# Forming the S5 way-in matrix in its final layout from turned B and repeated powers, in a one-layer hybrid encoder kernel

## Chip, cores and metric

One core of one Trainium2 chip runs the whole kernel. The metric is the device time of one execution in microseconds (us). Each kernel is run several times, and the median of the runs is its time.

## The reference

One encoder layer and a final RMS norm over 256 tokens of width 1024, all in f32. Cut to what matters here:

```python
q, k, v, u, g_a, g_s = split(rms_norm(h) @ w_in)          # 512 columns each for q, k, v, u; 1024 for g_a, g_s
o_a = diff_attention(rope(q), rope(k), v)                  # 4 heads, two softmaxes per head
o_s = s5_mixer(u)                                          # below
h = h + (sigmoid(g_a) * (o_a @ w_ba) + sigmoid(g_s) * (o_s @ w_bs)) @ w_mix_out
h = h + cross_attention(rms_norm(h), rms_norm(mem))        # 256 memory tokens
h = h + moe(rms_norm(h))                                   # top 4 of 32 experts, weights of 12.6 MB an expert

# s5_mixer, for each of 32 groups of 16 channels, 64 complex states, two directions:
ab = exp(a * dt); bb = ((ab - 1) / a) * b                  # bb: states x 16 channels
x[l] = ab * x[l-1] + bb @ u[l];  y[l] = real(c @ x[l])     # forward, and the same backward
```

## The kernel before

The kernel is written engine by engine: a block for SP (`block.sync`), for POOL (`block.gpsimd`), for PE, ACT and DVE, each a list of instructions in a fixed order. Semaphores tie them together, and nothing reorders an engine's list. So an instruction that waits holds up all that stands behind it on its engine.

Dense layers: a weight matrix comes in slabs of 512 columns. SP loads each in pieces of 512 rows (1 MB) into four slots of the tile `stage` (L307), and starts piece i when PE has used piece i-4 (`s_used`). The order is u, q, k, v, ga0, ga1, gs0, gs1 (the gates), mk0, mk1, mv0, mv1 (keys and values of the memory), and on to xo1. `natural` (L471) and `flipped` (L484) multiply a slab, in two layouts of the result. The results stand in four PSUM units PA to PD; `take` waits until the unit's last readers are done.

S5 works on chunks of 8 time steps: inside a chunk by a Toeplitz matrix (`toep`), between the 32 chunks by a scan on DVE. What a chunk adds to the state is `u` times the **way-in matrix** `lin`: for each group g a matrix of 128 rows (8 steps by 16 channels) and 256 columns (real and imaginary part of 128 states). Its entry is a power of `ab` for the step times `bb` for the channel. Before the change it is formed in five pieces of work:

1. `bbar` (states on partitions) from b and c by six DVE operations (L1366 to L1371), after rope of q and k.
2. For each of the 8 steps, six elementwise operations of 128x512 (`way_in_step`, L214) multiply `bbar` by one power into `s5b`, with the states on the partitions: 5 steps on DVE (`way_in`, L1405), 3 on POOL behind its own 48 operations for `s5w` (L399 to L404).
3. 64 transposes on PE (L460) turn `s5b`, 8 a PSUM unit. The units are PB and PD in turn.
4. ACT and DVE copy each turned unit back into the same place of `ring`, where it is now `lin`.
5. PE multiplies by it (L678).

In the same stretch PE runs the attention heads between the gate slabs: `scores(h)` (L596), then a gate slab during which DVE takes the row maxima (`row_max`, L1389), ACT the exponentials (`exps`, L1064) and DVE weighs the two softmaxes (`weigh`, L1394); then `turn_probs(h)` waits for `weigh(h)` (semaphore `pwv`), and `values(h)` for ACT's copy (`copy_probs`). The heads' order on PE is: scores 0, ga1, turn 0, scores 1, gs0, values 0, turn 1, scores 2, gs1, values 1, turn 2, scores 3, the matmuls of the taps (L654), values 2, the 64 transposes with turn 3 among them, values 3. `mem` is loaded by POOL after gs1 and normed into the tile of the first norm (`mn`).

On the DVE's list the way-in steps stand between the heads:

```python
            way_in(range(0, 1))
            for h, times in enumerate((range(1, 2), range(2, 3), range(3, WAY_IN_SPLIT), ())):
                row_max(h)
                weigh(h)
                if h == 0:
                    lag0()
                way_in(times)
```

`lag0` (L1414) forms the taps of lag 0 from a product of PE (L629). Behind the way-in matrix come the products (L678), their transposes, and the scan on DVE, which has to be done before PE's L719. From mk0 on the order of the program isn't touched by the change. The second half of the time is the mixture of experts: SP loads 192 chunks of 2 MB into a ring of 10 places, each when PE has used the chunk that was in its place.

## Time and profile before

| | us |
|---|---|
| median of 3 runs | 1316.97 |
| lowest and highest run | 1314.39, 1320.17 |
| the profiled execution, its own time | 1319.71 |
| its span, first to last instruction | 1317.9 |
| PE busy | 1262.1 (96%) |
| DVE, ACT, POOL busy | 348.2, 168.5, 109.6 |

The profile is of one execution. An engine's busy time says how long it worked, not whether it was waited for; the chain of waits says what released each piece of work up to the last. Times of day in the text are us from the span's start.

### The profile page before, as it was taken

The page shows a single profiled execution, that of the slowest core. Times are in us where ns is not written, and L with a number is a line of the kernel's source. Part 1 is how long each engine was busy: PE and PEld are TensorE (multiplying, and loading weights), DVE is VectorE, ACT ScalarE, POOL GpSimd, SP SyncE. Part 2 cuts the span into 40 slices and gives each one's busy share as a digit, 9 for nine tenths or more (in the row PEclk, how much of TensorE's full clock was granted, in tenths as well). Part 3 has the DMA queues.
Part 4 walks back from the last instruction along what each step waited for, and adds up shares of the span by engine and source line. Part 5 has one row for each costly group of instructions (what it writes and reads, how often), then busy time and mean ns, then how long its engine had stood idle before and what let it go on. Part 6 is the DMA issues. An engine that isn't in the chain of part 4 may idle for free.

```text
span 1317.9 us, 15237 instructions
## 1 busy us (share of the span) xinstructions
PE 1262.1 (96%) x6175; PEld 571.9 (43%) x6175; DVE 348.2 (26%) x754; ACT 168.5 (13%) x296; POOL 109.6 (8%) x108
## 2 busy tenths in 40 slices
PE   8999899999899999999999999999999999999996
PEld 3488785868653333333333333333333233333332
DVE  6578681121122111211122111211111112111112
ACT  2032422100311000000000000000000000000001
POOL 4699200010000000000000000000000000000000
PEclk9999999999989999999999999999999999999999
DMA  9633653549848999999999999999999999999994
GB/s 250 166 129 128 146 96 130 170 134 382 328 150 346 429 415 428 428 428 428 426 427 428 429 429 429 427 427 429 429 430 429 428 427 428 429 429 429 429 426 176
DMA packets 54984, 456.31 MB, mean 346 GB/s; under 512 B 4744, under 2 KB 6864, under 8 KB 30368
## 3 DMA queue, kind: packets, MB, share of 16 engines
q1 hardware_dynamic: 51744, 449.75, 82.9%
q0 software_dynamic: 2048, 5.47, 2.6%
q10 hardware_dynamic: 1152, 0.52, 0.3%
q8 instruction: 30, 0.49, 0.2%
q14 instruction: 10, 0.08, 0.0%
HBM read 453.59 MB, written 1.61 MB: 345 GB/s over the span
## 4 chain that ended last, share of the span: by engine, by line
PE 68%; DMA 23%; DVE 4%; ACT 3%; issue 1%; SPq 0%; ACTq 0%; DVEq 0%
PE pt L929 21%; PE pt L970 13%; DMA ring<-in_w_e 10%; DMA stage<-in_w_e 7%; DMA low<-in_w_e 6%; PE pt L493 6%; PE pt L480 6%; PE pt L528 4%; PE pt L866 4%; PE pt L460 3%; PE pt L851 3%; PE pt L541 2%; PE pt L923 1%; ACT wi_ L1008 1%; DMA stage<-in_w_in 1%; ACT low L1071 1%
## 5 line engine op out<-in xcount | busy, mean ns | idle before, releaser
L929 PE MATMUL pt<-ring,a 128*64 128x512 f32 x1216 | 273.0, 595 | 11.8 <-DMA ring<-in_w_e 11.7
L929 PEld LDWEIGHTS pt<-ring,a 128*64 128x64 f32 x1216 | 84.3, 137 | 193.4 <-issue 166.8
L970 PE MATMUL pt<-ring,wi_ 128*64 128x512 f32 x640 | 141.7, 595 | 4.6 <-ACT wi_ L1008 4.6
L1567 DVE COPY ct_<-ct_ 128x2 f32 x32 | 5.4, 170 | 468.7 <-PE pt L929 467.4
L929 PE MATMUL pt<-stage,a 128*64 128x512 f32 x416 | 95.3, 604 | 5.3 <-DMA stage<-in_w_e 5.3
L929 PE MATMUL pt<-low,a 128*64 128x512 f32 x416 | 93.8, 595 | 4.4 <-DMA low<-in_w_e 4.4
L970 PEld LDWEIGHTS pt<-ring,wi_ 128*64 128x64 f32 x640 | 44.6, 137 | 88.0 <-issue 82.0
L1184 ACT ACTIVATE hnt<-pt 128x512 f32<-128x512 f32 x32 | 19.1, 597 | 479.2 <-PE pt L929 479.2
L1644 DVE TENSOR_SCALAR hnt<-pt 128x512 f32<-128x512 f32 x32 | 22.1, 692 | 188.9 <-PE pt L929 188.9
L866 PE MATMUL pt<-hnt,lamb 64*128 64x512 f32 x256 | 65.3, 629 | 0.7 <-ACT hnt L1008 0.7
L851 PE MATMUL pt<-hres,ct_ 128*64 128x512 f32 x256 | 60.4, 592 | 0.0
L929 PEld LDWEIGHTS pt<-stage,a 128*64 128x64 f32 x416 | 29.1, 138 | 69.0 <-issue 58.4
L929 PEld LDWEIGHTS pt<-low,a 128*64 128x64 f32 x416 | 28.7, 137 | 67.3 <-issue 57.6
L480 PE MATMUL pt<-stage,hnt 128*128 128x512 f32 x128 | 55.3, 593 | 2.0 <-DMA stage<-in_w_in 2.0
L493 PE MATMUL pt<-hnt,stage 128*128 128x256 f32 x256 | 55.9, 379 | 0.0
L493 PEld LDWEIGHTS pt<-hnt,stage 128*128 128x128 f32 x256 | 48.6, 190 | 6.5
L1008 ACT ACTIVATE hnt<-pt 128x512 f32<-128x512 f32 (+1 forms) x34 | 21.1, 622 | 235.4 <-PE pt L970 230.3
L970 PE MATMUL pt<-low,wi_ 128*64 128x512 f32 x192 | 42.5, 595 | 1.3 <-ACT wi_ L1008 1.3
L970 PE MATMUL pt<-stage,wi_ 128*64 128x512 f32 x192 | 42.5, 595 | 1.3 <-ACT wi_ L1008 1.3
L1594 DVE TENSOR_TENSOR a<-pt,gains 128x512 f32<-128x512 f32 (+1 forms) x34 | 23.0, 676 | 70.2 <-PE pt L460 70.2
L480 PEld LDWEIGHTS pt<-stage,hnt 128*128 128x128 f32 x128 | 24.2, 190 | 31.8 <-issue 29.4
L923 PE MATMUL pt<-uT_,ct_ 32*64 32x512 f32 x256 | 34.8, 613 | 2.2 <-DMA low<-in_w_e 0.8
(325 smaller groups left out, 1215.4 us busy)
## 6 DMA issues: line engine op xcount, KB each, us to landing
ring<-in_w_e SPq DMA_DIRECT2D x116, 2048.0 KB, 35.9
low<-in_w_e SPq DMA_DIRECT2D x38, 2048.0 KB, 38.2
stage<-in_w_e SPq DMA_DIRECT2D x38, 2048.0 KB, 35.7
stage<-in_w_in SPq DMA_DIRECT2D x16, 1024.0 KB, 7.0
stage<-in_w_xkv SPq DMA_DIRECT2D x8, 1024.0 KB, 5.7
stage<-in_w_mix_out SPq DMA_DIRECT2D x4, 1024.0 KB, 5.1
stage<-in_w_xq SPq DMA_DIRECT2D x4, 1024.0 KB, 5.3
stage<-in_w_xo SPq DMA_DIRECT2D x4, 1024.0 KB, 16.5
```

The costliest lines, as they stand in the source:

```text
L460: return pe.transpose(dst, src, ident[0:n, 0:n])
L480: last = pe.matmul(pt[u][:, 512 * t:512 * t + 512], xT[:, k, t * P:(t + 1) * P], w[:, k % 4, :], start=(k == 0), stop=(k == 4 * len(ws) - 1))
L493: last = pe.matmul(pt[u][:, L * m:L * m + L], w[:, k % 4, m * P:(m + 1) * P], xT[:, k, :], start=(k == 0), stop=(k == 4 * len(ws) - 1))
L528: last = pe.matmul(pt[u][:, 512 * n:512 * (n + 1)], xT[:, k, P * t:P * (t + 1)], w[:, k % 4, :], start=(k == 0), stop=(k == KD - 1))
L541: last = pe.matmul(pt[u][:, L * m + P * t:L * m + P * (t + 1)], w[:, k % 4, m * P:(m + 1) * P], xT[:, k, P * t:P * (t + 1)], start=(k == 0 ...
L851: last = pe.matmul(pt[PD][SLOTS * n:SLOTS * (n + 1), 0:512], sel[:, t, :], h3[:, t, 512 * n:512 * (n + 1)], start=(t == 0), stop=(t == NT ...
L866: last = pe.matmul(pt[(PA, PB)[t]][:, 512 * n:512 * (n + 1)], gsc[SLOTS * n:SLOTS * (n + 1), t], ysb[SLOTS * n:SLOTS * (n + 1), :], start= ...
L923: pe.matmul(pt[PC][SLOTS * g:SLOTS * (g + 1), 512 * b:512 * (b + 1)], ecol[i:i + NE, :], be1[i:i + NE, :], start=False, stop=False)
L929: last = pe.matmul(pt[PC][SLOTS * g:SLOTS * (g + 1), 512 * b:512 * (b + 1)], xT[:, k % 4, k // 4], ring_slot[n][:, c:c + 512], start=(k == ...
L970: last = pe.matmul(pt[PD][SLOTS * h:SLOTS * (h + 1), 512:1024], hT[:, c, g], ring_slot[n][:, D * c + 512 * h:D * c + 512 * (h + 1)], start ...
L1008: return act.activation(dst, src, ACT.Copy)
L1594: return dve.tensor_tensor(xT[:, lo:hi], src, g3[:, lo:hi].to_broadcast([P, hi - lo, 2, SLOTS]), ALU.mult)
```

## The change

The way-in matrix is formed where PE wants it, with steps and channels on the partitions:

- **B turned once.** PE turns `bbar` (8 transposes, `turn_b`, into PD) in the middle of slab v, ACT copies it out (`b_turned`), and SP writes it to DRAM (`b_dram`, 0.5 MB).
- **Powers in row form.** The powers already stand on 32 partitions (one for each group). DVE copies them into order (`way_in_powers`, 4 copies and 4 memsets, behind rope of q), and SP writes them to DRAM in four transfers (`lam_dram`, 64 KB each), waits, and loads them back with **one DMA of 4 MB onto all 128 partitions**, straight into `lin`: each row of 32 KB is repeated on 16 partitions. That DMA stands ahead of ga0's pieces.
- **B repeated by DMAs.** Four loads of 1 MB (`load_b`) bring a quarter of turned B each, the same 16 rows repeated for the 8 steps, into two places of `ring`. The first two stand ahead of ga1's pieces, behind the write of `b_dram`; the third and fourth wait for quarters 1 and 2 of the matrix.
- **24 DVE operations of 128x1024** multiply the two in place, six a quarter. Six stand ahead of head 0, one between `row_max` and `weigh` of each head, and 0, 3, 7 and 4 behind the heads. POOL's 18 operations, DVE's 30 of 128x512, the 64 transposes and the 8 copies out of PSUM are gone.
- **DVE's order**: rope q, powers, `bbar`, rope k, lag 0, way-in. Lag 0's product on PE moves into slab v.
- **Heads up one slab.** Scores 0 run inside ga0, and each later step of a head one slab earlier; values 2 and turn 3 follow gs1. qT goes through PA, uT through PD.
- **The memory** is loaded by POOL once quarter 3 is done, into a piece of `ring`; its squares stand behind the exponentials of head 3. The Toeplitz loads wait also for the memory's transposes (`tokp`).
- Six semaphores are merged with others in the router and the first block of experts, with the same waits.

The diff, cut to its core:

```diff
@@ block.sync
+            def load_b(quarter):
+                src = b_dram[:, 2 * quarter:2 * quarter + 2].rearrange("h a n -> h (a n)").unsqueeze(0).to_broadcast([TC, HG, 2048])
+                dst = ring[:, 16384 + 2048 * (quarter % 2):16384 + 2048 * (quarter % 2 + 1)]
+                sp.dma_start(dst, src).then_inc(s_b[quarter % 2], 16)
             for i, (slab, w, r, c) in enumerate(SLOT_USES):
+                if i == SLAB_END["q"] + STAGE:
+                    sp.wait_ge(S["lamt"], 1)
+                    for j in range(4):
+                        sp.dma_start(lam_dram[:, :, j].rearrange("t a n -> a t n"),
+                                     lam_src[8 * j:8 * j + 8].rearrange("g t c m -> g t (c m)")).then_inc(s_tabw, 16)
+                    sp.wait_ge(s_tabw, 4 * 16)
+                    sp.wait_ge(S["taba"], 1)
+                    powers = lam_dram.rearrange("t a j n -> t (a j n)").unsqueeze(1).to_broadcast([TC, HG, 8 * 8 * P])
+                    sp.dma_start(lin_flat, powers).then_inc(s_lam, 16)
+                if i == SLAB_END["k"] + STAGE:
+                    sp.wait_ge(S["bte"], 1)
+                    sp.dma_start(b_dram.rearrange("h a n -> a h n"), b_turned).then_inc(s_tabw, 16)
+                    sp.wait_ge(s_tabw, 5 * 16)
+                    load_b(0)
+                    sp.wait_ge(S["rope"], 2)
+                    load_b(1)
+                if i == SLAB_END["v"] + STAGE:
+                    sp.wait_ge(S["lin"], 1)
+                    load_b(2)
+                if i == SLAB_END["ga1"] + STAGE:
+                    sp.wait_ge(S["lin"], 2)
+                    load_b(3)
@@ block.gpsimd
-            for t in range(WAY_IN_SPLIT, TC):
-                last = way_in_step(pool, t, tmp_p, link)
-            slab_done(pool, "gs1")
+            pool.wait_ge(S["lin"], 3)
             pool.dma_start(mn, T["mem"].rearrange("a (t p) n -> p (a t) n", p=P)).then_inc(s_mem, 16)
@@ block.tensor
-            natural("v", PB, hnT, ("vev", 1))
+            natural("v", PB, hnT, ("vev", 1), inside={(0, 4): turn_b, (1, 0): lag0_products})
-            pe.wait_ge(S["bp"], 2)
-            for r in range(8):
-                u, read = ((PB, "lta"), (PD, "ltv"))[r % 2]
-                take(u, (read, r // 2 + 1))
-                for i in range(8):
-                    last = turn(pt[u][:, P * i:P * (i + 1)], s5b[:, 4 * r + i // 2, i % 2])
-                last.then_inc(S["ltp"], 1)
-                if r == 1:
-                    turn_probs(3)
@@ block.vector
+            def way_in():
+                for q in range(4):
+                    rows = b_rows[q % 2]
+                    lr, li = (lin[:, 2 * q:2 * q + 2, :, c].rearrange("p a j m -> p (a j) m") for c in range(2))
+                    br, bi = rows[:, :, 0], rows[:, :, 1]
+                    dve.wait_ge(s_b[q % 2], 16 * (q // 2 + 1))
+                    if q == 0:
+                        dve.wait_ge(s_lam, 16)
+                        dve.wait_ge(S["bspl"], 1)
+                    dve.tensor_tensor(way_a, lr, br, ALU.mult)
+                    dve.tensor_tensor(way_c, lr, bi, ALU.mult)
+                    link(dve.tensor_tensor(bi, li, bi, ALU.mult))
+                    dve.tensor_tensor(lr, way_a, bi, ALU.subtract)
+                    link(dve.tensor_tensor(br, li, br, ALU.mult))
+                    dve.tensor_tensor(li, way_c, br, ALU.add).then_inc(S["lin"], 1)
+                    dve.wait_ge(S["lin"], q + 1)
-            way_in(range(0, 1))
-            for h, times in enumerate((range(1, 2), range(2, 3), range(3, WAY_IN_SPLIT), ())):
+            lag0()
+            some_way_in(6)
+            for h, (between, behind) in enumerate(((1, 0), (1, 3), (1, 7), (1, 4))):
                 row_max(h)
+                some_way_in(between)
                 weigh(h)
-                if h == 0:
-                    lag0()
-                way_in(times)
+                some_way_in(behind)
```

How the instructions stand now, at three places. On PE from slab k (L480 before; now from the 8 transposes inside slab v, L497) to the first use of head 0's probabilities; `L460`/`L475` are transposes, `L601`/`L638` scores, `L493`/`L512` a gate slab of 32 matmuls, `L629`/`L610` the product for lag 0. Before:

```order
L480 MATMUL pt<-stage,hnt 128x512 x32
L460 MATMUL pt<-con,a 128x128 x8
L493 MATMUL pt<-hnt,stage 128x256 x32
L460 MATMUL pt<-con,low 128x128 x16
L629 MATMUL pt<-ct_,ring 128x128 x8
L601 MATMUL pt<-low 128x256
L601 MATMUL pt<-big,low 128x256
L601 MATMUL pt<-low 128x256
L601 MATMUL pt<-big,low 128x256
L493 MATMUL pt<-hnt,stage 128x256 x32
L460 MATMUL pt<-con,low 128x128 x4
```

And now:

```order
L475 MATMUL pt<-con,ring 128x128 x8
L497 MATMUL pt<-stage,hnt 128x512 x4
L610 MATMUL pt<-ct_,ring 128x128 x8
L497 MATMUL pt<-stage,hnt 128x512 x8
L475 MATMUL pt<-con,a 128x128 x8
L475 MATMUL pt<-con,low 128x128 x16
L512 MATMUL pt<-hnt,stage 128x256 x8
L638 MATMUL pt<-low 128x256
L638 MATMUL pt<-big,low 128x256
L638 MATMUL pt<-low 128x256
L638 MATMUL pt<-big,low 128x256
L512 MATMUL pt<-hnt,stage 128x256 x24
```

Eight transposes and the lag-0 product have moved into slab v, and head 0's scores stand after a quarter of ga0, so `turn_probs(0)` (the last row before, and the row behind these now) comes one gate slab earlier: behind ga0 instead of ga1.

On PE behind the last gate slab (before from the taps' 64 matmuls, now from the slab's own 32) to the product with the way-in matrix (L678 before, L702 now). Before:

```order
L654 MATMUL pt<-ring 32x128 x64
L620 MATMUL pt<-low 128x128 x4
L460 MATMUL pt<-con,ring 128x128 x16
L460 MATMUL pt<-con,low 128x128 x4
L460 MATMUL pt<-con,ring 128x128 x48
L620 MATMUL pt<-low 128x128 x4
L678 MATMUL pt<-ring,uT_ 32x256 x32
```

And now:

```order
L512 MATMUL pt<-hnt,stage 128x256 x32
L657 MATMUL pt<-low 128x128 x4
L475 MATMUL pt<-con,low 128x128 x4
L475 MATMUL pt<-con,ring 128x128 x8
L691 MATMUL pt<-ring 32x128 x64
L657 MATMUL pt<-low 128x128 x4
L702 MATMUL pt<-ring,uT_ 32x256 x32
```

The 64 transposes of `ring` are gone; 8 of the memory have come in, with the last head's probabilities ahead of the taps (L654, L691).

On SP's queue: before from the gains' loads to behind the taps' writes, now from the first weight piece to them ( `8x8x256` and the like are the shape written):

```order
L296 DMA ring<-in_norm_mix_g 8x128
L296 DMA ring<-in_norm_mem_g 8x128
L296 DMA ring<-in_norm_cross_g 8x128
L307 DMA stage<-in_w_in 128x4x512 x16
L307 DMA stage<-in_w_xkv 128x4x512 x4
L302 DMA taps_dram<-low 16x8x128 x8
L307 DMA stage<-in_w_xkv 128x4x512 x4
```

```order
L330 DMA stage<-in_w_in 128x4x512 x8
L302 DMA lam_dram<-ring 8x8x256 x4
L307 DMA ring<-lam_dram 128x1x8192
L330 DMA stage<-in_w_in 128x4x512 x2
L310 DMA b_dram<-ring 8x16x1024
L296 DMA ring<-b_dram 128x1x2048 x2
L330 DMA stage<-in_w_in 128x4x512 x2
L296 DMA ring<-b_dram 128x1x2048
L330 DMA stage<-in_w_in 128x4x512 x4
L296 DMA ring<-b_dram 128x1x2048
L330 DMA stage<-in_w_xkv 128x4x512 x4
L325 DMA taps_dram<-low 16x8x128 x8
```

Nine transfers have come in between the weight pieces; pieces 9 to 16 stand behind them.

## Rows read from the trace of the kernel before

**Rows 1.** The page: what the DMA moved, in 40 slices of 32.9 us.

```profile
GB/s 250 166 129 128 146 96 130 170 134 382 328 150 346 429 415 428 428 428 428 426 427 428 429 429 429 427 427 429 429 430 429 428 427 428 429 429 429 429 426 176
```

**Rows 2.** Chain of waits, PE, slabs k to ga0: start us, us, what.

```profile
42.89 27.47 PE pt L480 x64
70.36 0.87 PE pt L460 x8
71.23 13.83 PE pt L493 x64
...
89.00 2.01 PE pt L601 x8
```

**Rows 3.** Timeline of PE: start us, us, line, out<-in, count [idle before].

```profile
86.63 1.95 PE L629 MATMUL pt<-ct_,ring 128*128 128x128 f32 x16
...
137.49 1.05 PE L620 MATMUL pt<-low 128*128 128x128 f32 x8
...
140.64 3.70 PE L654 MATMUL pt<-ring 128*32 128x128 f32 x128
...
148.18 3.38 PE L460 MATMUL pt<-con,ring 128*128 128x128 f32 x16 [2.75 <-ACT low L1008]
...
161.75 3.66 PE L678 MATMUL pt<-ring,uT_ 128*32 128x256 f32 x64 [0.47 <-issue]
...
170.53 27.89 PE L493 MATMUL pt<-low,stage 128*128 128x256 f32 x128 [1.48 <-DVE low L1232]
```

**Rows 4.** Windows: busy of PE, PEld, DVE, ACT, POOL; clock; DMA share, GB/s.

```profile
145.00:148.00 3.00, 0.43 (x4) 0.24 (x3) 1.63 (x8) 2.49 (x7) 0.00 (x0) 0.96 0.28 100
148.00:151.50 3.50, 3.32 (x17) 3.35 (x18) 0.44 (x4) 0.04 (x1) 0.00 (x0) 0.55 0.64 97
...
155.50:158.00 2.50, 2.24 (x17) 1.71 (x16) 1.23 (x1) 2.32 (x4) 2.50 (x5) 1.00 1.07 146
```

**Rows 5.** Timeline of DVE, same columns.

```profile
35.38 0.74 DVE L1332 COPY low<-ring 32x512 f32<-32x512 f32 x2
...
45.42 1.27 DVE L1351 TENSOR_TENSOR low<-ring 128x256 f32<-128x256 f32 x1
...
103.48 1.43 DVE L219 TENSOR_TENSOR ring<-ring,wi_ 128x512 f32<-128x512 f32 x1
...
111.03 1.23 DVE L1391 TENSOR_REDUCE sm<-pt 128x4 f32<-128x1024 f32 x1
112.29 1.00 DVE L1392 TENSOR_SCALAR sm<-sm 128x4 f32<-128x4 f32 x1
...
116.35 2.01 DVE L1401 SCALAR_TENSOR_TENSOR low<-low,sm 128x256 f32<-128x256 f32 x2 [0.58 <-ACT low L1075]
...
134.46 0.69 DVE L219 TENSOR_TENSOR ring<-ring,wi_ 128x512 f32<-128x512 f32 x1
...
171.84 1.22 DVE L1460 TENSOR_TENSOR low<-low 128x1024 f32<-128x1024 f32 x1
```

**Rows 6.** Chain of waits, ACT's part of head 1.

```profile
113.32 1.94 ACT low L1071 x8
...
115.80 0.52 ACT low L1075
```

**Rows 7.** Timeline of POOL, the last of its 48 operations for s5w.

```profile
105.91 1.60 POOL L404 TENSOR_TENSOR ring<-ring 128x512 f32<-128x512 f32 x1
```

**Rows 8.** DMA issues, 0 to 350 us: KB each, median us to landing.

```profile
stage<-in_w_xo SPq DMA_DIRECT2D x4, 1024.0 KB, 16.5
...
stage<-in_w_glu SPq DMA_DIRECT2D x2, 1024.0 KB, 5.0
...
taps_dram<-low SPq DMA_DIRECT2D x8, 64.0 KB, 2.1
```

**Rows 9.** DMA, 150 to 180 us: the Toeplitz loads.

```profile
GB/s 146 139 133 113 3 0 0 109 257 93 87 131 93 104 93 109 93 93 131 98 109 93 93 120 87 131 93 87 126 93 93 109 82 38 5 0 0 0 0 0
```

**Rows 10.** Timeline of SP: the issue of ga0's first piece.

```profile
53.22 0.37 SPq L307 DMA_DIRECT2D stage<-in_w_in  x1
```

More of the change, by code:

```diff
@@ L469, in weights, with natural @@
                 return got
[L471 removed]
+            def natural(slab, u, xT, *who, inside=None):
                 ws = weights(slab)
@@ L488, in flipped @@
                 for m in range(4):
+                    if inside and m in inside:
+                        inside[m]()
                     for k in range(4 * len(ws)):
@@ L622, in values, with scores_of_first_head @@
                 last.then_inc(S["pvp"], 1)
-            pe.wait_ge(S["bspl"], 1)
-            take(PA, ("kse", 1))
-            for j in range(4):
-                for c in range(2):
-                    last = pe.matmul(pt[PA][:, P * j:P * (j + 1)], bbar[:, c, 8 * j:8 * j + 8], ct[:, c, j],
-                                     start=(c == 0), stop=(c == 1))
-            last.then_inc(S["k0p"], 1)
-            pe.wait_ge(S["qka"], 2)
-            pe.wait_ge(S["vev"], 1)
-            scores(0)
-            flipped("ga1", PB, hnT, ("gates", 2))
+            def scores_of_first_head():
+                pe.wait_ge(S["qka"], 2)
+                pe.wait_ge(S["vev"], 1)
+                scores(0)
+            flipped("ga0", PB, hnT, ("gates", 1), inside={1: scores_of_first_head})
             turn_probs(0)
             scores(1)
-            flipped("gs0", PB, hnT, ("gates", 3))
+            flipped("ga1", PB, hnT, ("gates", 2))
             values(0)
@@ L645, in _ @@
             scores(3)
+            flipped("gs1", PB, hnT, ("gates", 4))
+            values(2)
+            turn_probs(3)
+            turn_some(mn, 0, PD, 1)
             pe.wait_ge(S["s5wd"], 1)
@@ L1109, in _ @@
             act.wait_ge(S["kse"], 1)
-            copy(ring[:, 22528:23552], unit(PB)).then_inc(S["zka"], 1)
-            for i, u in enumerate((PB, PD)):
+            copy(ring[:, 22528:23552], unit(PD)).then_inc(S["zka"], 1)
+            for i, u in enumerate((PD, PB)):
                 act.wait_ge(S["ztp"], i + 1)
@@ L1333, in _, with way_in_powers @@
             last.then_inc(S["tabsrc"], 1)
+            def way_in_powers():
+                for c in range(2):
+                    dve.tensor_copy(lam_src[:, 0:TC - 1, c, 0:NS], pwn[:, c, TC - 2::-1, 0:NS])
+                    dve.tensor_copy(lam_src[:, 1:TC, c, NS:P], pwn[:, c, 0:TC - 1, NS:P])
+                    dve.memset(lam_src[:, TC - 1, c, 0:NS], 1.0 - c)
+                    last = dve.memset(lam_src[:, 0, c, NS:P], 1.0 - c)
+                last.then_inc(S["lamt"], 1)
             cos = con[:, C_COS:C_COS + NT * 32].rearrange("p (t i) -> p t i", t=NT)
```

214 lines of the change are left out of this document (99 added, 115 removed).

## Prediction

> **What bounds the kernel now.** I read the page first. PE is busy almost everywhere, and from slice 14 on the DMA moves 427 to 430 GB/s [rows 1]: the experts' weights. Each of those loads waits for PE to use an earlier chunk, so the second half starts when PE gets there and then takes its own time. The change touches nothing in it but names of semaphores. Time is won or lost ahead of mk0, and only by moving the moment when PE starts it: 170.53 [rows 3]. So the chain of waits and PE's timeline up to there are what counts.
>
> In them PE has no gap to speak of from slab k to the first scores: k and v take 27.5 us, ga0 13.8, eight transposes 0.87, the four score products 2.0 at most [rows 2]. The gaps are behind gs1. Head 3's weighing is late, and PE stands for 2.75 us, then for 0.47 and 1.48 more [rows 3]; between them each unit of 8 transposes waits for the copy of an earlier one. After the first gap the granted clock is 0.55, about the lower of PE's two levels (1.2 of 2.4 GHz), and 16 transposes take 3.38 us [rows 3, 4] where two times 0.87 would do: 1.6 us lost.
>
> DVE is the second thing to see. An operation of 128x512 with both inputs in SBUF takes 1.43 us at 103 us and 0.69 us at 134 us [rows 5]. The first stands beside POOL's operations for s5w, which end at 107.5 [rows 7] and are followed by POOL's way-in steps; the second stands alone. POOL beside it costs DVE 0.74 us an operation.
>
> **What the change takes off PE.** From the end of gs1 (137.5) to mk0 (170.5) are 33.0 us [rows 3]. Values 1, turn 2 and scores 3 (0.9 + 0.4 + 1.8 = 3.1) now stand ahead of gs1, which leaves 29.9. In their place the new order has: values 2 0.9, turn 3 0.4, eight transposes of the memory 0.9, the taps 3.7, values 3 0.9, the product with the way-in matrix 3.7 [rows 3], eight transposes of the memory 0.9, sixteen of the product 1.8: 13.2 us, with each copy between them behind other work of PE. That is 16.7 us less: 56 transposes, the low clock and all the gaps. Earlier, `turn_b` adds 0.9 inside slab v, and 0.4 us of waiting ahead of the first scores goes, since a quarter of ga0 now covers ACT's copies. **The gain is 16.2 us**, if nobody makes PE wait anew.
>
> **What it adds.** The critical new wait is `turn_probs(0)`. PE gets there at 70.36 [rows 2] + 0.9 (`turn_b`) + 1.9 (the lag-0 product, rows 3) = 73.1 at the end of v; + 0.9 + 1.75 for uT, q and k = 75.7; + 13.8 for ga0 and 1.8 for the scores = 91.4. It needs head 0's weighing. On DVE that now stands behind six way-in operations, and those stand behind a relay of DMAs:
>
> - Rope of q ends at 46.7 [rows 5]. Four copies of 32x448: 0.37 us each alone (the copies of 32x512), at most 1.27 each beside POOL [rows 5]; I take 0.6, since most copies of this size are short, and 0.1 for each memset: 49.5. Bounds 48.6 and 52.2.
> - Four writes of 64 KB: four issues of 0.4 [rows 10], the last lands in 2.1 [rows 8]: 53.2. Only then is the load of the powers issued, ahead of ga0's pieces.
> - A piece of 1.05 MB alone lands in 5.0 us [rows 8]; at 428 GB/s [rows 1] it moves for 2.45. So 2.5 us are fixed, half ahead of the data and half behind.
> - The powers are 4.19 MB. **No row shows such a transfer.** From above: 428 GB/s, as the experts' chunks, 9.8 us. From below: the Toeplitz loads, 2.1 MB in about 20 us, 105 GB/s [rows 9], 40 us. The fast loads all have 128 rows outermost on both sides. I take this half: rows of 32 KB have nothing of the small pieces that make the Toeplitz loads slow. Powers: 53.2 + 1.3 + 19.6 = 74.1.
> - Transfers on one queue pass behind each other: the pieces of xo, issued behind six chunks, land in 16.5 us instead of 5.0 [rows 8]. So ga0's two pieces move until 79.0 (landed 77.7 and 80.2: PE waits 2 to 3 us for them, which the later wait swallows), the write of turned B (0.52 MB, ready since 62) until 81.5, done at 82.7, and only then is quarter 0 issued: 82.7 + 1.3 + 4.9 + 1.2 = **90.1**.
>
> The Trainium skill, "DMA: Bandwidth & Descriptors", section "Why a DMA increments its semaphore by 16 and not by 1", says that the number of engines is the largest up to 16 that divides both sides' slowest dimension; for 8 against 128 that is 8. By it the sum is the one with 214 GB/s, without it the one of the first rival; no run here shows it yet.
>
> From 90.1 DVE needs: six operations of 128x1024, 1.22 alone [rows 5] + 0.74 beside POOL, which still works then, + 0.1 between them, 12.3; row maximum and its small one 2.3 [rows 5]; the seventh operation 2.05, beside ACT's exponentials of 1.94 [rows 6]; reciprocal and factor 0.5; ACT's scaling 0.6 [rows 6]; weighing 2.0 [rows 5]. Together 19.7, so 109.8: PE waits 18.4 us in all, and 1.6 for the low clock behind the gap (as in rows 4; from nothing to twice that) make **20.0 us**.
>
> Hidden: `bbar`, 8.8 us of DVE, is done at 58, and slab v reaches its first quarter at 60. Rope of k ends by 65.5, lag 0 by 71, PE's transposes of k come at 75. B's loads 2 and 3 move while DVE works on a quarter loaded before; the pieces of ga1 are issued at 83 and needed at 114. In heads 1 to 3 the DVE has 16.9 us from scores to scores (gate slab 13.8, values 0.9, turn 0.4, scores 1.8). It needs most in head 2: row maximum 1.4, exponentials 1.9, 0.5 + 0.6 + 0.9 and seven operations of 1.25, 14.1. Head 3's four operations end 10.3 us behind its scores, the memory is normed by 13, PE wants it at 15. One copy of 1.2 us now stands ahead of the scan, behind which PE has mk0 and mk1, 27.9 us [rows 3]: nothing, or 1.2 if that cover is short.
>
> **Sum.** -16.2 + 20.0 = +3.8 us. The profiled execution, 1319.7, would become 1323.5. It lies 2.7 over the median of the runs, so I give the median plus 3.8: **1321 us**. Put shortly, the result is what is left of the time at which quarter 0 lands, less 86.3.
>
> **Rivals.**
>
> 1. *The loads run at the full rate.* For it: every long load of this trace does. Then the powers move till 64.3, the pieces till 69.2, turned B is written at 71.6, quarter 0 lands at 76.6, weighing ends at 96.3. PE waits 4.9, with the clock 6.5: 9.7 us faster, 1307. Chance 0.22.
> 2. *DVE's queue is late in every head*, the slower side. The spare is 2.8 us in head 2 and 2 in head 3. If the operations stay near 2.05 us after POOL has ended (operands in strides of 256, new shapes), the eight of head 2 cost 6.4 more, 3.6 over the spare, and head 3's four 3.2, 1.2 over: 4.8 us on top, 1326 (8.6 over the time before). It decides from 1.6 us an operation. Against it: widths and types are those of the 1.22 us row. Chance 0.12.
> 3. *Repeated reads are slow* like the Toeplitz loads. Quarter 0 lands at 118; POOL is done by then, so 13.2 us behind it; PE waits 40: 25 us slower, 1342. It is slower by over 0.5% from a rate of about 195 GB/s down. Chance 0.08.
> 4. *The change doesn't do what it says*: PE's transposes were cover for DVE's chain, which is the same length after all, and nothing moves: 1317. Against it: the chain passes through PE and its low clock behind 148 [rows 3, 4]. Chance 0.03.
>
> **Chances and range.** The forecast has 0.55; its own range is 1316 to 1327 (quarter 0 from 87 to 95, clock and scan), with a tenth of all beyond +6.6. A measurement of this kernel can tell about 0.5%, 6.6 us, from no change. Faster than that: 0.19, from rival 1. Slower: 0.10 of the forecast, 0.09 of rival 2, 0.08 of rival 3, 0.27. Within: 0.54. The range 1305 to 1330 leaves out rival 3 and the edges of 1 and 2, about 0.15.
>
> **What would show it.** In the profile after: the powers' DMA landing about 22 us behind its issue (12 with rival 1) with a DMA share near one half; the first way-in operation near 90; one gap of PE of 15 to 18 us ahead of the first `turn_probs`, with a clock below 1 behind it; way-in operations of 2 us and later 1.25; no gap of more than 1 us from gs1 to mk0, 13 to 14 us apart; mk0's start near 174. I am wrong if the gap is at another place, if it is below 8 us, or if the time from mk0 to the end differs by more than 2 us from the 1147 of before.

## The result, and the profile after

| | before | changed |
|---|---|---|
| median of 4 runs, us | 1318.57 | 1351.98 (1348.37 to 1352.63) |
| ratio to before | | 1.0253 [1.0233, 1.0273] |
| profiled execution, us | 1319.71 | 1348.37 |
| its span, us | 1317.9 | 1346.6 |
| PE busy / waits of PE, 60 to 210 us | 1262.1 / 7.1 | 1254.8 / 44.2 |
| start of mk0, us | 170.53 | 203.05 |
| from mk0 to the end, us | 1147.4 | 1143.5 |

The change makes the kernel 33 us slower; 1321 was forecast. PE has less to do and stands still for 37 us more. The profiled execution of the changed kernel is the fastest of its four, so the two spans lie only 28.7 us apart. The page of the changed kernel shows where: clock, share of the DMA engines and what they moved, in 40 slices of 33.7 us.

```profile
PEclk9967899999998999999999999999999999999999
DMA  8756659444965999999999999999999999999995
GB/s 245 153 112 142 204 185 174 141 138 161 416 239 201 405 429 419 427 428 427 428 427 428 428 428 428 428 428 428 428 428 428 429 428 429 428 429 428 428 428 217
```

From slice 15 on it reads like [rows 1]: the experts' half is what it was. In slices 3 and 4 (67 to 135 us) the granted clock is down, which happens where PE idles, and slice 3 moved 112 GB/s. PE's timeline there (columns as in [rows 3]):

```profile
74.09 1.91 PE L475 MATMUL pt<-con,low 128*128 128x128 f32 x16
105.31 6.35 PE L512 MATMUL pt<-hnt,stage 128*128 128x256 f32 x16 [29.30 <-DMA stage<-in_w_in]
...
113.22 10.52 PE L512 MATMUL pt<-hnt,stage 128*128 128x256 f32 x48
138.66 1.12 PE L475 MATMUL pt<-con,low 128*128 128x128 f32 x4 [14.91 <-DVE low L1417]
...
189.76 1.05 PE L657 MATMUL pt<-low 128*128 128x128 f32 x8
...
192.05 3.70 PE L691 MATMUL pt<-ring 128*32 128x128 f32 x128
...
196.77 3.67 PE L702 MATMUL pt<-ring,uT_ 128*32 128x256 f32 x64
200.37 2.84 PE L475 MATMUL pt<-con,ring 128*128 128x128 f32 x24
203.05 3.19 PE L512 MATMUL pt<-low,stage 128*128 128x256 f32 x14
```

There are two gaps, 29.3 us ahead of ga0 and 14.9 ahead of `turn_probs(0)` (L475, four transposes). Behind the first, 16 matmuls took 6.35 us, with a granted clock of 0.53 from 105 to 111 us; the same 16 take 3.62 in the run quarters, where no gap stands ahead of them. From there to mk0 nothing waits: from the end of gs1 (189.76) to mk0 (203.05) are 13.3 us, where [rows 3] had 33.0.

What held them is in SP's timeline and in a window of the whole core (columns as in [rows 4]). SP's timeline:

```profile
52.10 2.17 SPq L302 DMA_DIRECT2D lam_dram<-ring  x4
56.53 0.72 SPq L307 DMA_DIRECT2D ring<-lam_dram  x1
57.29 1.00 SPq L330 DMA_DIRECT2D stage<-in_w_in  x2
62.38 0.60 SPq L310 DMA_DIRECT2D b_dram<-ring  x1
110.23 1.21 SPq L296 DMA_DIRECT2D ring<-b_dram  x2
...
132.55 0.59 SPq L296 DMA_DIRECT2D ring<-b_dram  x1
```

The window:

```profile
80.00:100.00 20.00, 0.00 (x0) 0.00 (x0) 0.00 (x0) 0.00 (x0) 18.68 (x17) 0.50 0.49 106
```

The powers' load (L307) is issued at 56.5, ga0's two pieces at 57.3, the write of turned B at 62.4. From 80 to 100 us, while the powers move, the mean busy share of the 16 DMA engines is 0.49, what eight busy engines give, and together they bring 106 GB/s. At that rate 4.19 MB are 39.5 us. ga0's pieces stand behind it on the queue, and so does the write of B. The chain of waits says it in four lines; its second DMA is the load of quarter 1, issued with quarter 0 and landed at 135.5:

```profile
62.38 47.83 DMA b_dram<-ring
...
110.87 24.67 DMA ring<-b_dram
...
138.61 0.04 issue
138.66 1.12 PE pt L475 x4
```

And DVE's timeline: the copies that make the powers' table, and the first way-in operation.

```profile
46.95 1.37 DVE L1345 COPY ring<-ring 32x448 f32<-32x448 f32 x1
...
125.37 1.23 DVE L1431 TENSOR_TENSOR ring<-ring 128x1024 f32<-128x1024 f32 x1 [51.80 <-DMA ring<-b_dram]
...
135.57 1.22 DVE L1431 TENSOR_TENSOR ring<-ring 128x1024 f32<-128x1024 f32 x1 [1.58 <-DMA ring<-b_dram]
```

DVE idles 51.8 us for quarter 0, which lands at 125.4; 90.1 was forecast. The last row is the seventh operation, between head 0's maximum and weights. It waits 1.58 us for quarter 1, and that wait ends last ahead of `turn_probs(0)`. The prediction had it at nothing.

### The profile page after: what moved, and what is told of

It reads as the page before. It is cut to its first block, busy times and chain, and to the rows that moved or that the text cites. A ratio compares the mean times of both kernels' runs of the same rounds, so it can differ in the third digit from the quotient of the medians.

```text
span 1346.6 us, 15102 instructions
## 1 busy us (share of the span) xinstructions
PE 1254.8 (93%) x6119; PEld 565.5 (42%) x6119; DVE 335.6 (25%) x744; ACT 165.7 (12%) x293; POOL 83.3 (6%) x90
## 4 chain that ended last, share of the span: by engine, by line
PE 66%; DMA 31%; ACT 2%; DVE 1%; issue 0%; SPq 0%; ACTq 0%; DVEq 0%
PE pt L948 19%; PE pt L989 13%; DMA ring<-in_w_e 12%; PE pt L512 8%; DMA stage<-in_w_e 6%; DMA low<-in_w_e 6%; PE pt L497 5%; PE pt L547 4%; DMA b_dram<-ring 4%; PE pt L888 3%; PE pt L873 3%; PE pt L475 3%; PE pt L560 2%; DMA ring<-b_dram 2%; PE pt L942 1%; ACT wi_ L1027 1%
## 5 line engine op out<-in xcount | busy, mean ns | idle before, releaser
L512 PE MATMUL pt<-hnt,stage 128*128 128x256 f32 x256 | 58.8, 392 | 29.3 <-DMA stage<-in_w_in 29.3
L512 PEld LDWEIGHTS pt<-hnt,stage 128*128 128x128 f32 x256 | 50.5, 198 | 36.8 <-issue 29.5
L497 PE MATMUL pt<-stage,hnt 128*128 128x512 f32 x128 | 55.7, 593 | 2.2 <-DMA stage<-in_w_in 2.2
L948 PEld LDWEIGHTS pt<-low,a 128*64 128x64 f32 x416 | 28.7, 137 | 67.3 <-issue 57.6
L989 PE MATMUL pt<-stage,wi_ 128*64 128x512 f32 x192 | 42.5, 596 | 1.3 <-ACT wi_ L1027 1.3
L989 PE MATMUL pt<-low,wi_ 128*64 128x512 f32 x192 | 42.5, 596 | 1.3 <-ACT wi_ L1027 1.3
L497 PEld LDWEIGHTS pt<-stage,hnt 128*128 128x128 f32 x128 | 24.0, 190 | 31.1 <-issue 28.7
```

The source lines that it names most:

```text
L497: last = pe.matmul(pt[u][:, 512 * t:512 * t + 512], xT[:, k, t * P:(t + 1) * P], w[:, k % 4, :], start=(k == 0), stop=(k == 4 * len(ws) - 1))
L512: last = pe.matmul(pt[u][:, L * m:L * m + L], w[:, k % 4, m * P:(m + 1) * P], xT[:, k, :], start=(k == 0), stop=(k == 4 * len(ws) - 1))
L948: last = pe.matmul(pt[PC][SLOTS * g:SLOTS * (g + 1), 512 * b:512 * (b + 1)], xT[:, k % 4, k // 4], ring_slot[n][:, c:c + 512], start=(k == ...
L989: last = pe.matmul(pt[PD][SLOTS * h:SLOTS * (h + 1), 512:1024], hT[:, c, g], ring_slot[n][:, D * c + 512 * h:D * c + 512 * (h + 1)], start ...
```

## The experiments

The theory: these loads run at a quarter of the full rate, because of how their rows are dealt out over engines and partitions; what stands behind them on the queue comes late, and through it PE. Rivals were that the repeated reading of a row is slow, that DVE's order is the cause, and that the queue's order alone is. Each expectation says what its theories A, B and so on are.

### dma_shapes: the loads by themselves

A kernel with nothing but loads from the experts' weights, each awaited before the next (it computes nothing of the reference), in one execution. All but the last move 2.1 MB:

```
own_a   128 rows, one per partition
rep_b   8 rows, each onto 16 partitions (the powers' shape)
own_c   8 blocks of 16 different rows (the shape of one quarter of B)
rep_d   16 rows, each onto 8            rep_e   32 rows, each onto 4
rep_f   1 row onto 128                  blocks_g  8 loads of 16 partitions
part_h  8 rows onto 32 partitions, 0.5 MB
```

> Not the layer: only loads of 2.1 MB (16 KB a partition), each alone on SP's queue, its landing awaited, and x copied to the output. a: 128 rows, each its own. b: 8 rows, each 16 times, as the powers of the change. c: 8 groups of 16 rows, all different, with the groups as outermost count. d: 16 rows, each 8 times. e: 32 rows, each 4 times. f: one row 128 times. g: eight loads of 16 partitions from one row each. h: 8 rows, each 4 times, onto 32 partitions (0.5 MB). Rival B (repeated reads of one row are slow): a and c 7.5, b, d, e, f slow, f the slowest, h 7.4. Rival C (only the count of engines, 8 of 16, each at half rate for another reason): b and c 21.5, d 7.5, h 7.4.

SP's timeline: each issue stands where the load before it had landed.

```profile
5.12 0.33 SPq L32 DMA_DIRECT2D own_a<-in_w_e  x1
12.36 0.77 SPq L34 DMA_DIRECT2D rep_b<-in_w_e  x1
34.34 0.60 SPq L36 DMA_DIRECT2D own_c<-in_w_e  x1
56.08 0.59 SPq L38 DMA_DIRECT2D rep_d<-in_w_e  x1
68.12 0.58 SPq L40 DMA_DIRECT2D rep_e<-in_w_e  x1
75.79 0.34 SPq L42 DMA_DIRECT2D rep_f<-in_w_e  x1
82.80 3.59 SPq L45 DMA_DIRECT2D blocks_g<-in_w_e  x8
102.44 0.74 SPq L47 DMA_DIRECT2D part_h<-in_w_e  x1
107.22 0.85 SPq L50 DMA_DIRECT2D out_dram<-xs  x2
```

Windows of three of them, rep_b, blocks_g and part_h (busy of POOL, the only other engine with a record; clock; DMA share; GB/s):

```profile
13.00:34.00 21.00, 0.00 (x0) 1.00 0.46 100
...
83.00:102.00 19.00, 0.00 (x0) 1.00 0.90 110
...
104.50:106.00 1.50, 0.00 (x0) 1.00 0.48 197
```

The differences of the first column: own_a 7.2 us, rep_b 22.0, own_c 21.7, rep_d 12.0, rep_e 7.7, rep_f 7.0, blocks_g 19.6, part_h 4.8. **Repeating is not what is slow**: one row onto 128 partitions is as fast as 128 rows, and 8 blocks of different rows are as slow as 8 repeated rows.
### both_128 and powers_128: the same program, fast loads

The loads' sources become 128 rows of an expert's weights, in powers_128 for the powers alone. S5 is then computed from other numbers; all instructions, sizes and waits stay, and from mk0 to the end both take 1145.5 us, as the runs with the layer's own numbers do (1144.6 to 1145.6).

```diff
-                    powers = lam_dram.rearrange("t a j n -> t (a j n)").unsqueeze(1).to_broadcast([TC, HG, 8 * 8 * P])
+                    powers = T["w_e1"][0, 0].rearrange("(p r) n -> p (r n)", p=P)[:, 0:8192]
-                src = b_dram[:, 2 * quarter:2 * quarter + 2].rearrange("h a n -> h (a n)").unsqueeze(0).to_broadcast([TC, HG, 2048])
+                src = T["w_e1"][0, 1].rearrange("(p r) n -> p (r n)", p=P)[:, 2048 * quarter:2048 * (quarter + 1)]
```

> The powers and the four quarters of B are loaded from as many bytes of the experts' weights, with 128 rows outermost (so the S5 branch is computed from other numbers); all waits stay. Theory A: the powers land about 12 us behind their issue, ga0's pieces by 75, quarter 0 at 82 instead of 125, head 0 is weighed at 102, PE waits some 10 us ahead of turn 0 and none ahead of ga0: 44 us of gaps become 10, the time is 3 to 8 us below that of before. Rival (the relay of writes and waits on SP is what costs, not the rate): PE still waits over 30 us and the time stays 20 us or more above before.

> The powers alone are loaded from 128 rows of the experts' weights; B as in the change. Theory A: no wait ahead of ga0, quarter 0 lands at 89 to 92, PE waits 17 to 20 us ahead of turn 0; the time within 5 us of before, some 30 us below the change. Rival (B's loads cost as much as the powers): still 15 us or more above before.

both_128 took 1316.35 us, ratio 0.9987 [0.9978, 0.9997]; powers_128 1324.96, 1.0055 [1.0038, 1.0072]. The gap ahead of ga0 is gone in both. What is left of PE's waits is one line in each, `turn_probs(0)` (us in total, times, longest). both_128:

```profile
PE pt L475 <- DVE low L1417: 10.2, 1, 10.2
```

powers_128:

```profile
PE pt L475 <- DVE low L1417: 18.7, 1, 18.7
```

The first way-in operation starts at 82.8 and 91.5. So 27 of the 33 us go with the rate of one load, the powers', and 36 with both. Quarter 0 and the waits came as expected in both, the times did not quite: both_128 is 1.3 us below its own before (3 to 8 were expected), powers_128 7.3 above it (at most 5). powers_128 is the nearest to the forecast of the change itself: quarter 0 at 91.5 for 90.1, and +7.3 us for +3.8.

### ga0_first: the queue's order alone

SP issues ga0's pieces ahead of the powers, by waiting for the table's write one place later (the load of the powers stands behind that wait and moves with it):

```diff
-                    sp.wait_ge(s_tabw, 4 * 16)
+                if i == SLAB_END["k"] + STAGE:
+                    sp.wait_ge(s_tabw, 4 * 16)
```

> The change with ga0's two pieces issued ahead of the load of the powers. If the sum is set by the landing of quarter 0 alone, the gap of 29 us ahead of ga0 goes and the one ahead of turn 0 grows from 15 to some 44: the time stays that of the change within 3 us. Rival (the two gaps add up because ga0's pieces come late): 20 us or more below the change.

1345.47 us, 1.0205 [1.0182, 1.0228], between the two expectations (within 3 us of the changed kernel, or 20 below it) and near the first. The 29 us gap ahead of ga0 vanished, and the one at `turn_probs(0)` grew from 14.9 to 38.2. Of the 29 us just 6.5 were won, by what quarter 0 landed earlier (117.8 for 125.4). The first gap was real, but it lay in the shadow of the second.

### late: way-in behind the heads

```diff
-            some_way_in(6)
-            for h, (between, behind) in enumerate(((1, 0), (1, 3), (1, 7), (1, 4))):
+            for h, (between, behind) in enumerate(((0, 0), (0, 9), (1, 8), (1, 5))):
```

> The changed kernel with its loads as they are, and with the first quarter's six operations moved out of VectorE's way ahead of head 0: no way-in operation stands before head 0's maximum and weights, and the quarters are worked off behind heads 0 to 3 (9, 9 and 6 operations). Theory A (the whole loss comes from when quarter 0 lands, and it is felt at turn_probs(0) only because VectorE's queue puts the weights behind that quarter): the gap ahead of ga0 stays at 29 us, the 14.9 us wait at turn_probs(0) goes, quarter 0 still lands at 125 us, and quarter 2, issued at 133 us after quarter 0 is used, now holds gs0's pieces back, so a gap of 6 to 10 us appears ahead of gs0, which is then due at 144 us. Time 1340 to 1346 us, 6 to 12 us below the changed kernel. Theory B (the head's own chain, scores to weights beside POOL's program, is what turn_probs(0) waits for, and the loads only happen to end then): the wait at turn_probs(0) stays over 8 us, and the time stays within 3 us of the changed kernel.

1350.19 us, 1.0242 [1.0226, 1.0257]: a miss. The wait at `turn_probs(0)` went, as theory A had it, yet nothing was won. PE's timeline:

```profile
105.78 6.58 PE L512 MATMUL pt<-hnt,stage 128*128 128x256 f32 x16 [29.51 <-DMA stage<-in_w_in]
...
138.24 16.08 PE L512 MATMUL pt<-hnt,stage 128*128 128x256 f32 x64 [11.62 <-DMA stage<-in_w_in]
```

I had looked for the new gap ahead of gs0 at most. It is ahead of ga1, whose pieces are issued at 112 behind two quarters of B. In the changed kernel they came as late (27.7 us after issue, 27.2 here), hidden under the wait at `turn_probs(0)`.

### quarters and quarters_nb: the powers in four loads

One load of 1.05 MB ahead of each quarter of B; quarters_nb also moves head 0's one operation behind its weights.

```diff
-                    sp.dma_start(lin_flat, powers).then_inc(s_lam, 16)
+                    load_powers(0)
...
                     load_b(0)
+                    load_powers(1)
...
+                    load_powers(2)
                     load_b(2)
...
+                    load_powers(3)
                     load_b(3)
```

> The changed kernel with the powers' 4.2 MB load cut into four loads of 1.05 MB, one ahead of each quarter of B; tables, shapes and VectorE's order stay. Theory A (each of these loads runs at about 110 GB/s, and the queue passes everything behind it on no faster, so what stands ahead of quarter 0 sets turn_probs(0)): the first quarter of the powers lands near 67 us, ga0's pieces 10 us behind it (gap ahead of ga0 0 to 6 us instead of 29), B's write lands near 80 us and quarter 0 at 98 to 103 us instead of 125; turn_probs(0) waits 15 to 22 us and runs near 112 us instead of 139. The last quarter's two loads come later relative to PE, which may give 0 to 12 us back ahead of the memory part. Time 1320 to 1334 us. Theory B (a load that repeats rows costs a fixed time per load, or the rate falls with every load in flight): quarter 0 lands after 115 us, and the time stays above 1340 us.

> quarters with one operation moved: the way-in operation that stands between head 0's maximum and its weights (it waited until 115.5 us for quarter 1 and so held turn_probs(0) until 118.6 us) goes behind the weights. If what decides is when the pieces of PE's slabs get through the queue behind the way-in's loads, turn_probs(0) runs 7 to 9 us earlier, near 111 us, and ga1 with it, but gs0's pieces land at 145 us as in quarters: its gap grows from 5.7 to 12 to 15 us, and the time stays within 3 us of quarters (1347 to 1353 us). If it is VectorE's order, the 8 us are won: 1340 to 1343 us.

quarters: 1349.69 us, 1.0234 [1.0218, 1.025]. quarters_nb: 1352.28, 1.0243 [1.0216, 1.027]. The loads did as theory A expected, or better: no gap ahead of ga0, quarter 0 used from 94.1 (98 to 103 were expected). The time did not: 1320 to 1334 was expected, a miss by 16 us. DVE's timeline of quarters, from head 0's row maximum on:

```profile
106.58 1.23 DVE L1414 TENSOR_REDUCE sm<-pt 128x4 f32<-128x1024 f32 x1
107.84 0.78 DVE L1415 TENSOR_SCALAR sm<-sm 128x4 f32<-128x4 f32 x1
115.52 1.22 DVE L1437 TENSOR_TENSOR ring<-ring 128x1024 f32<-128x1024 f32 x1 [6.89 <-DMA ring<-b_dram]
```

The operation between maximum and weights waits for quarter 1, and the weights stand behind it. quarters_nb took it away, `turn_probs(0)` came 4.8 us earlier (113.8; near 111 was expected), and PE waited longer for the pieces of ga1 and gs0 instead (10.4 us for 5.7; 7.7 of them ahead of gs0, where 12 to 15 were expected). Its time is inside the expected 1347 to 1353. The waits of PE sum to 44.2 us in the changed kernel, 42.5 in late, 44.9 in quarters, 41.7 in quarters_nb. I read that as one shortage in four places: powers and B are 8.4 MB, 79 us at 106 GB/s, on the queue on which PE's slabs stand. No run shows it by itself, and v3_narrow, below, gets the waits down to 32.4 us with the same loads in another order.

### ceiling: fast loads and way-in behind the heads

both_128 with the order of late (S5 from other numbers again).

> Powers and B taken from 128 rows of an expert's weights (S5 is then computed from other numbers), as in both_128, and the way-in behind the heads as in late: what the regrouped program would take if neither the loads' rate nor VectorE's order held the first head up. Theory A (the reordering itself, heads one slab up and memory ahead, gives the 16 us of the prediction, and the two waits are all that stands against it): no gap ahead of ga0, no wait over 2 us at turn_probs(0), the memory part's first matmul at 157 to 161 us, time 1304 to 1310 us, 8 to 14 us below the kernel before. Theory C (the 16 us were mostly shifted, not won: something behind the memory part gives them back): the memory part starts as early, but the time stays at 1314 us or more.

1312.05 us, 0.9946 [0.9931, 0.9961]. `turn_probs(0)` waits for nothing, but gs0's pieces, issued once quarter 0 is used (113 us), make a gap of 8.3 us. The expectation of 1304 to 1310 had missed that queue, and mk0 starts at 167.5 where 157 to 161 was expected.

### v3 and v3_narrow: wider loads

v3 writes the powers' table twice over (16 rows, each onto 8 partitions) and B's too (32 rows, loaded onto 32 partitions at a time), loads the powers in quarters, issues ga0's and ga1's pieces ahead of them, and has the way-in behind the heads. v3_narrow has the same order with the changed kernel's shapes. Between the two lies this, beside the second copies of the tables:

```diff
-                powers = lam_dram[:, 2 * quarter:2 * quarter + 2].rearrange("t a j n -> t (a j n)").unsqueeze(1).to_broadcast([TC, HG, 2048])
+                powers = lam_dram[:, :, 2 * quarter:2 * quarter + 2].rearrange("t d a j n -> (t d) (a j n)").unsqueeze(1).to_broadcast([2 * TC, HG // 2, 2048])
...
-                src = b_dram[:, 2 * quarter:2 * quarter + 2].rearrange("h a n -> h (a n)").unsqueeze(0).to_broadcast([TC, HG, 2048])
-                dst = ring[:, 16384 + 2048 * (quarter % 2):16384 + 2048 * (quarter % 2 + 1)]
-                sp.dma_start(dst, src).then_inc(s_b[quarter % 2], 16)
+                src = b_dram[:, 2 * quarter:2 * quarter + 2].rearrange("h a n -> h (a n)")
+                for j in range(4):
+                    dst = ring[32 * j:32 * (j + 1), 16384 + 2048 * (quarter % 2):16384 + 2048 * (quarter % 2 + 1)]
+                    sp.dma_start(dst, src).then_inc(s_b[quarter % 2], 16)
```

> A version meant to be fast with the reference's numbers: the powers' table is written twice over (16 rows, each repeated onto 8 partitions, which took 12.0 us for 2.1 MB by itself) and loaded in quarters; B's table is written twice over (32 rows) and each quarter is loaded by four loads of 32 partitions; ga0's pieces are issued ahead of the powers, ga1's ahead of B; the way-in stands behind the heads. If loads onto 32 neighbouring partitions from 32 rows run at 200 GB/s or more (theory A: what counts is how many groups of partitions the engines write at the same time), a quarter of B lands 10 us after issue, no gap ahead of ga0 or gs0 passes 4 us, quarter 3 is in place before PE wants it, and the time is 1306 to 1314 us, below the kernel before by 4 to 12 us. If they run at 110 GB/s, quarter 3 is late by 10 to 20 us and the time is 1318 to 1330 us.

> v3 with the shapes of the loads as in the changed kernel (the powers' table once, 8 outermost rows repeated 16 times; B's quarter as one load of 8 blocks of 16 partitions), in v3's order of loads and of VectorE's work, the powers in quarters. Theory A (of v3's gain over the changed kernel nearly all comes from the loads' width, and the order alone cannot help, because 8.4 MB at 110 GB/s are 76 us of a queue that PE's slabs stand in too; late and quarters each moved one wait and got it back at the next place): the gap is 20 to 40 us in all, mostly PE waiting for pieces of slabs behind loads of the way-in, the last quarter lands after 170 us, and the time is 1338 to 1356 us. Theory D (the order did it: ga0's and ga1's pieces ahead and the way-in behind the heads are enough): the time is below 1325 us.

v3: 1314.75 us, 0.9984 [0.9969, 0.9998]. v3_narrow: 1337.22, 1.0139 [1.0124, 1.0154]. Order alone (with the powers in quarters) is worth 14.8 us against the changed kernel, the width of the loads another 22.5. Theory A of v3_narrow had given the order nothing; it missed the time by 0.8 us and the last quarter, which was in use from 166 us and not after 170. PE's waits in v3_narrow:

```profile
PE pt L484 <- DVE low L1426: 13.7, 1, 13.7
PE pt L521 <- DMA stage<-in_w_in: 11.3, 1, 11.3
PE pt L484 <- DVE ring L1242: 7.4, 1, 7.4
```

And in v3:

```profile
PE pt L487 <- DVE ring L1245: 7.9, 1, 7.9
PE pt L524 <- DMA stage<-in_w_in: 1.0, 1, 1.0
PE pt L487 <- DVE low L1429: 0.6, 1, 0.6
```

v3 ended just above its expected 1306 to 1314: from 80 to 100 us its DMA engines are busy throughout (share 0.99) with 180 GB/s, below the 200 of its theory A. The powers and pieces of slabs move in the same window, so the rate of the loads onto 32 partitions by themselves is not known. The wait for DVE L1245 is for the normalised memory; v3_narrow has it as L1242. The memory is loaded once quarter 2 is used and landed at 145.7, and PE turns it ahead of everything else.

### v4 and v6: the memory out of the way

v4 puts the turns of the memory behind the taps' products, and the normalisation on DVE into the middle of quarter 3. v6 also puts ACT's squares of the memory behind gs1's gate copy. The lines are those of v4 against v3.

```diff
             turn_probs(3)
-            turn_some(mn, 0, PD, 1)
...
             last.then_inc(S["kp"], 1)
+            turn_some(mn, 0, PD, 1)
...
-            for h, (between, behind) in enumerate(((0, 0), (0, 9), (1, 8), (1, 5))):
+            for h, (between, behind) in enumerate(((0, 3), (0, 9), (0, 6), (0, 0))):
...
-            chunk_factors()
+            some_way_in(3)
             normed(1, mn, mn)
+            some_way_in(3)
+            chunk_factors()
```

> v3 with two moves: PE's first turns of the normalised memory go behind the taps' products instead of ahead of them (in v3 PE stood 7.9 us in front of them, for memory had landed only at 145.7 us and the normalisation stood behind the last way-in operations on VectorE), and VectorE does three operations of quarter 0 behind head 0, none inside a head, and the normalisation of memory in the middle of quarter 3. Expected: no wait of PE over 3 us between 76 and 168 us, the first matmul on memory's keys at 160 to 163 us (167.84 in v3), time 1306 to 1310 us (ceiling took 1312.1 us with an 8.3 us gap of its own). Against it: if quarter 0 lands later than 96 us, its three operations hold head 1's maximum up and a gap of 1 to 4 us appears at turn_probs(1); then 1310 to 1314 us.

> v4 with ScalarE's squares and root of the normalised memory moved behind gs1's gate copy and head 3's transposed weights: in v4 the gate copy, and with it bank B, which the taps' products need, stood behind the landing of memory, and PE waited 5.1 us for it, with the 128 products then at the low clock (6.13 us instead of 3.70). Expected: that wait under 1 us, the products at 145 to 146 us in 3.7 us, then a wait of 0 to 3 us for the normalisation ahead of memory's turns; the first matmul on memory's keys at 159 to 163 us (164.84 in v4), time 1306 to 1310 us. If memory lands so late that only the place of the wait changes, the time is that of v4, 1311 to 1312 us.

v4: 1311.55 us, 0.9943 [0.9929, 0.9957]. v6: 1311.5, 0.9954 [0.9936, 0.9971]. Both are about 0.5% faster than the kernel before, and alike. Both missed 1306 to 1310 by 1.5 us and the start of mk0 by 1 to 2 (164.8 and 164.1); v4's 1310 to 1314 for a quarter 0 behind 96 us came true (96.3), but the wait was another than it said: 5.1 us for ACT. PE's waits in v4:

```profile
PE pt L702 <- ACT a L1039: 5.1, 1, 5.1
PE pt L524 <- DMA stage<-in_w_in: 1.3, 1, 1.3
PE pt L714 <- DVE low L1251: 0.6, 1, 0.6
```

And in v6:

```profile
PE pt L714 <- DVE low L1251: 3.8, 1, 3.8
PE pt L487 <- DVE ring L1245: 2.6, 1, 2.6
PE pt L524 <- DMA stage<-in_w_in: 1.4, 1, 1.4
```

ACT's wait is gone in v6, and 6.4 us of waiting for the memory have taken its place: the case in which only the place of the wait changes. 3.8 of them are DVE's order: the product with the gains (L1251) stands behind the last three way-in operations and starts at 155.1, though PE had turned the memory by 151.8. An earlier load of the memory, or that product further up, would be next; neither was tried.

## Why the prediction was wrong

**The step that failed** is the rate of the powers: "I take this half: rows of 32 KB have nothing of the small pieces that make the Toeplitz loads slow", 214 GB/s. The count of engines was right (share 0.49 in the window above, 0.46 in rep_b), the rate of each was not: 106 GB/s in all for 214, as the Toeplitz loads' 105 [rows 9], whose slowness I had put down to small pieces. What I had left out is where those engines write: the same half of the engines brought 197 GB/s onto blocks of 4 partitions (part_h) and 100 onto blocks of 16 (rep_b). The bound from below was the true value. Nearly everything downstream is this one term:

| | forecast | measured |
|---|---|---|
| powers issued | 53.2 | 56.5 |
| PE's gap ahead of ga0 | 2 to 3 | 29.3 |
| turned B written | 82.7 | 110.2 |
| quarter 0 in place | 90.1 | 125.4 |
| from there to the end of weighing | 19.7 | 13.2 |
| end of gs1 to mk0 | 13.2 | 13.3 |
| mk0 to the end | 1147.4 | 1143.5 |

- *The copies* took 1.06 to 1.41 us each, not 0.6: beside POOL all of them were slow. The table was ready at 52.0, inside the bounds of 48.6 and 52.2, and the powers were issued 3.3 us late.
- *The relay* was right but for its last link: table, write, powers, pieces, B's write, quarter 0, six operations, and then quarter 1 (1.6 us), weights, `turn_probs(0)`. By its own sign of being wrong the prediction failed: it had one gap, ahead of `turn_probs(0)`, and the larger one, 29.3 us, stood ahead of ga0. The rule "landing of quarter 0, less 86.3" can be tried on four kernels, against the span of before. both_128: 82.8 gives -3.5, measured -3.8. powers_128: 91.5 gives +5.2, measured +2.8. ga0_first: 117.8 gives +31.5, measured +24.3. The changed kernel: 125.4 gives +39.1, measured +28.7. It holds while POOL still works. By 105 us POOL is done and the six operations take 7.2 us for 12.3, which is 5.1 of the 7 to 10 us of difference. Spans are single executions; by the medians the four are -1.3, +7.3, +27.8 and +33.4, and with the 5.1 us taken off for the last two (26.4 and 34.0) the rule is within 2.2 us of each. It no longer holds for late, where DVE's order is another.
- *The gain* was about right in size. Span less PE's waits is 1310.8 us before and 1302.4 in the changed kernel, and 1301.5 to 1305.8 in the others (quarters_nb: 1311.9). With the 7.1 us of waiting that before has, that is 12 to 16 us of the 16.2. But 2 to 4 of them lie behind mk0, where nothing was forecast; ahead of mk0 they are 9 to 14 (quarters_nb: 4), with what the low clock costs behind the gaps still in them. v4 realises 8.3 us in the span (6.9 by the medians). The rest is new waiting of 7.0 us.
- *Heads 1 to 3* never stall PE in the changed kernel, as said (head 3 does in quarters, 5.6 us, and in v3_narrow, 13.7, where quarter 3 is late); operations beside POOL took 2.07 us (quarters) and alone 1.22.
- *Rival 3* was what happened, with a chance of 0.08: it had quarter 0 at 118 and 13.2 us behind it, and +25. Its mechanism (repeated reads) was not the true one; rep_f refutes it. The rate it assumed was, by luck.
- *The check on mk0 to the end* (within 2 us of 1147.4) failed too, by 3.9 us less. All eleven runs of the layer's variants have 1144.6 to 1145.6, wherever their mk0 starts, so some 2 us lie in the changed order, and 1 to 2 more in that execution. Why is open.

Nothing in the trace of before forbade the right answer. The Toeplitz loads [rows 9] fill 16 neighbouring partitions each, just as blocks_g does, and I explained them away. Taken as the nearest row in shape, their 105 GB/s would have put the forecast at rival 3's 1342.

## What to carry to other kernels

The rate of a load hangs on how its outermost dimension spreads over engines and over partitions, and not on repeated reads: here 8 outermost with 16 neighbours each ran at 100 to 106 GB/s, 8 with 4 neighbours each at 197, and 32 outermost at the full rate. Before a large load goes ahead of weights on one queue, take its rate from a row that fills partitions in the same blocks, and add up the bytes that the queue must move by each deadline; moving one wait may only show the next if that sum is too large (42 to 45 us in four arrangements, 32 in a fifth). A wait that ends last hides others of nearly its size, so price all consumers of the late queue, and let no operation that needs a load stand inside a chain that PE waits for.

## What the hardware did that I had not expected

- 8 blocks of 16 partitions keep half of the engines busy (share 0.46) and bring 100 GB/s; 8 blocks of 4 with the same share (0.48) bring 197. With nearly all engines busy (0.90) inside 16 partitions it is 110 GB/s.
- 16 rows onto 8 partitions each took 12.0 us for 2.1 MB, 32 rows onto 4 each 7.7, one row onto all 7.0, 128 rows 7.2.
- A narrow load holds up the pieces behind it though half of the engines are idle: ga0's two pieces, issued 0.8 us behind the powers, landed 48 and 50 us after their issue. From 57 to 80 us the share is 0.86, from 80 to 100 it is 0.49. That reads as if the other eight engines had done their part of the pieces by 80 us, and the pieces waited for the part of the eight that move the powers; no run shows it by itself.
- Copies within SBUF of 32x448 took 1.06 to 1.41 us beside POOL; 32x512 takes 0.37 while POOL rests [rows 5].
